# Moving the wait for the gate-bias transfers from behind the first token tile to ahead of the tile loop on VectorE

## The reference, cut to what matters

```
h = rmsnorm(x, norm1_g) * (1 + mod[:, 1]) + mod[:, 0]
p = h @ w_in + b_in            # columns: q, k, v, o (512 each), 16 gates, fourier (512)
...
gates = p[..., OFF_G:OFF_F]    # i and f pre-activations, two directions x four heads
...                            # mLSTM heads, Fourier heads, w_out, expert-choice MoE, final norm
```

## Time and profile before

| what | value |
|---|---|
| median of 3 runs | 2356.2 us (2352.03 to 2357.64) |
| the profiled execution's own time | 2357.64 us |
| its span in the trace | 2355.8 us |
| PE busy | 2190.1 us (93%) |
| DVE busy | 490.4 us (21%) |
| ACT busy | 358.3 us (15%) |
| POOL busy | 271.0 us (12%) |
| mean granted TensorE clock | 0.968 |

### The profile page before, as it was taken

The page is one execution under the profiler, slowest core; times in us unless marked ns, Lnnn a source line. Parts: engine busy times, 40 slices in busy tenths (PEclk is TensorE's granted clock), DMA queues, the critical chain, the costliest instruction groups (busy, mean ns, idle before and its releaser), DMA issues. The chain is left out here.

```text
span 2355.8 us, 37038 instructions
## 1 busy us (share of the span) xinstructions
PE 2190.1 (93%) x15013; PEld 1892.5 (80%) x15013; DVE 490.4 (21%) x1246; ACT 358.3 (15%) x1012; POOL 271.0 (12%) x266
## 2 busy tenths in 40 slices
PE   7999999859985399999999999999999999999992
PEld 2445554846553399999999999999999999999992
DVE  1111115167774410101011101010111011101102
ACT  1011112313321011101111111011111110111102
POOL 0000000011120102022021020120210201202102
PEclk9999999989998699999999999999999999999996
DMA  9720101163422677697797976977979869779775
GB/s 377 294 99 31 62 31 45 72 241 132 137 91 102 205 251 239 245 363 219 277 325 225 345 245 244 363 218 272 330 224 341 250 243 363 218 268 335 224 255 179
DMA packets 351601, 528.76 MB, mean 224 GB/s; under 512 B 12996, under 2 KB 292284, under 8 KB 348232
## 3 DMA queue, kind: packets, MB, share of 16 engines
q1 hardware_dynamic: 336456, 509.35, 62.4%
q0 software_dynamic: 15104, 18.88, 3.9%
HBM read 492.23 MB, written 35.95 MB: 224 GB/s over the span
## 5 line engine op out<-in xcount | busy, mean ns | idle before, releaser
L1626 PE MATMUL ps_ab<-xeT,ring 128*128 128x144 f32 x8192 | 1009.2, 286 | 14.7 <-DVE xeT L1671 14.7
L1626 PEld LDWEIGHTS ps_ab<-xeT,ring 128*128 128x128 f32 x8192 | 1007.5, 190 | 14.8 <-issue 14.8
L1639 PE MATMUL ps_yy<-hidT,ring 128*128 128x144 f32 x4096 | 504.4, 286 | 0.0
L1639 PEld LDWEIGHTS ps_yy<-hidT,ring 128*128 128x128 f32 x4096 | 502.8, 190 | 0.0
L463 PE MATMUL ps_p<-w_in_sb,hT 128*128 128x512 f32 x720 | 318.1, 595 | 3.0 <-DMA w_in_sb<-in_w_in 3.0
L1675 DVE TENSOR_TENSOR hidT<-silu,ps_ab 128x144 f32<-128x144 f32 x256 | 77.8, 304 | 887.0 <-ACT silu L1593 824.7
L463 PEld LDWEIGHTS ps_p<-w_in_sb,hT 128*128 128x128 f32 x720 | 134.6, 191 | 156.6 <-issue 155.5
L1572 POOL DMA_INDIRECT stream<-ye,slot_row x64 | 101.0, 1578 | 1216.5 <-DVE ye_p L1686 1201.9
L1593 ACT ACTIVATE silu<-ps_ab 128x144 f32<-128x144 f32 x256 | 74.5, 291 | 909.8 <-PE ps_ab L1626 884.4
L1215 PE MATMUL b_z<-y,mixT 128*128 128x512 f32 x288 | 129.7, 604 | 10.3 <-ACT aff L1149 10.3
L1679 DVE STREAM_TRANSPOSE yS<-yT 128x1024 f32<-128x1024 f32 x16 | 19.9, 1245 | 457.3 <-ACT yT_p L1600 457.3
(11 more groups left out here) (250 smaller groups left out, 1082.3 us busy)
## 6 DMA issues: line engine op xcount, KB each, us to landing
ring<-in_exp_w SPq DMA_DIRECT2D x384, 1024.0 KB, 12.3
y<-in_ada_w SPq DMA_DIRECT2D x22, 1024.0 KB, 8.1
w_in_sb<-in_w_in SPq DMA_DIRECT2D x4, 2048.0 KB, 21.5
kv<-kvo SPq DMA_DIRECT2D x15, 512.0 KB, 5.7
kvo<-pr SPq DMA_DIRECT2D x9, 768.0 KB, 3.3
qkT_dram<-qkT SPq DMA_DIRECT2D x9, 512.0 KB, 4.8
qk<-qkT_dram SPq DMA_DIRECT2D x9, 512.0 KB, 5.1
m_in<-m_lanes SPq DMA_DIRECT2D x9, 512.0 KB, 5.8
```

What stands on the lines that cost most here:

```text
L1626: mm = nc.tensor.matmul(ps_ab[f % 2][:, N * w:N * w + N], unit[:, k, bass.ts(c, P)], xeT[:, k], start=(k == 0), stop=(k == DT - 1))
L1639: mm = nc.tensor.matmul(ps_yy[d % 2][:, 0:N], unit[:, f % 2, bass.ts(d, P)], hT[:, f], start=(f == 0), stop=(f == FT - 1))
```

## The change

VectorE's wait for the four `b_gate` transfers stood in the body of tile 0, behind its five block additions and just ahead of `keep_gates`. It is taken from there and put ahead of the tile loop, before the wait for `b_in_row`. No instruction is added or removed, and nothing on any other engine or queue is changed.

```diff
                     if only(i, 0):
-                        dve.wait_ge(bg_loaded, 16 * 4)
                         keep_gates()
...
                 keep_shift(ps_ada, 1, 0)
                 g.dve.settle()
                 keep_h(0, 0)
+                dve.wait_ge(bg_loaded, 16 * 4)
                 dve.wait_ge(g.b_in_loaded, 16)
                 tile_loop(dve, g.dve, body, {"hT_ready_dve": 8, "block_kept": 10, "x_normed": 2, "gates_kept": 2})
```

## The result

The changed kernel took 2374.11 us (median of 4 runs, 2371.6 to 2375.61), the kernel before 2354.79 us beside it. The ratio is 1.0081, with a 95% interval of 1.0063 to 1.0098: 0.8% slower, clear of no change. A second set of runs of the same two kernels (in the experiments) gave 1.0067 (1.0050 to 1.0084).

A forecast was written before the change was run, and what follows sets the result against it. The prediction took TensorE's nearly unbroken input projection (1.4 us of waits after 32.09 us) as the bound. Stall 16.4 + clock 2.3 = 18.7 us, on the median 2356.2, gave 2375 us, range 2368 to 2381.

The forecast's parts named there:

- The old place costs nothing: Wait in tile 0's body: keep_gates at 75.03 is released by PE's gate product, so removing the wait gains 0.
- The landing: When the four b_gate transfers on SP's queue have landed: 63.0 us, with 62.5 and 65.4 as ends.
- The group of 46 small packets: Packets under 512 B at 60.2 to 61.0 us, read as the close of the constants together with the four b_gate transfers.
- 2 us behind the closing packets: A transfer counts as landed some 2 us after its closing packets, as the first ada_w slice did at 65.4.
- The stall: PE waits before turn(0) of tile 0 for the first addition: start at 64.0 in place of 47.60, 16.4 us.
- The clock: PE restarts at the lower clock level after the idle time in tile 0: 2.3 us lost, ends 1.6 and 3.0.
- What is late next: SP's first store and the ada_w slices behind it move with the stall; no further cost or gain in the stage: 0.
- The sum: Whole kernel: 16.4 + 2.3 = 18.7 us, forecast 2375 us, 0.8% slower; chance 0.83.
- That small transfers are not held up by the queue: Rival on SP's queue: the four land at 53.1, stall 6.5 us plus 2.3 for the clock, 2365.0 us; chance 0.07.
- That they land with the slices behind them: Rival on SP's queue: completion held up to 72.8 us, stall 26.2 us, time 2384.7 us; chance 0.05.
- The hidden wait: Rival at tile 0's first addition: biases landed by 46.6 us, cost 0, time 2356.2 us; chance 0.03.
- The stall given back: Rival in the stage: something going on during PE's stall absorbs up to 18.7 us; 2373.5 at best, no separate chance.

The follow-up runs named there:

- e7: The kernel before, wait at its old place, with the four bias transfers issued ahead of the w_in blocks; ratio 0.9996.
- e4: The changed kernel with the four bias transfers issued behind the four ada_w slices; ratio 1.0106.
- e5: The changed kernel with the four bias transfers issued just ahead of the 1.5 MB of constants; ratio 1.0053.
- e6: The changed kernel with the bias transfers issued by ACT on its own queue, behind its part of the first hT tile (about 31 us); ratio 0.9996.
- e2: The changed kernel with the wait moved behind the first of the five block additions, so the second is held; ratio 1.0044.
- e3: The changed kernel with the wait moved behind the second of the five block additions, so the third is held; ratio 1.0005.
- e8: The changed kernel with 16 spare 128x512 matmuls, result unread, ahead of turn(0) of tile 0, inside PE's wait; ratio 1.0062.
- e9: The changed kernel with the bias transfers issued by ACT on its own queue only when PE has ended block 1; one run, 2360.86 us.
- e10: The changed kernel run and profiled once more, no edit; ratio to the kernel before 1.0067.
- e1: The changed kernel with the four bias transfers issued ahead of the w_in blocks (about 12.7 us); ratio 0.9996.
- e11: The kernel before run and profiled once more, no edit; one run, 2357.59 us.

## Why the prediction held, point by point

**The old place costs nothing.** Held: `keep_gates` is released by the gate product in both kernels, and in e7 the transfers are issued at 12.6 in place of 50.35 us, with no change of time.

**The landing (forecast 63.0, ends 62.5 to 65.4).** It was 62.1, 0.9 us sooner and below the lower end. The constants landed at 44.41 + 18.4 = 62.8, 0.7 us behind the four small transfers issued after them. The prediction had put them next to the constants and allowed at most 0.5 us for landing ahead. The group of 46 small packets was read rightly: in the changed kernel they come from 60.6 to 61.1, in e4 from 70.5 to 71.0 and in e5 from 57.0 to 57.5, and each time the addition starts some 1.0 to 1.1 us behind them. What was off is the "2 us behind the closing packets", taken from a transfer of 1 MB: it is half of that for the small ones. The groups of e4 and e5:

```profile
DMA packets 50, 0.02 MB, mean 50 GB/s; under 512 B 47, under 2 KB 47, under 8 KB 47
...
DMA packets 101, 0.25 MB, mean 508 GB/s; under 512 B 45, under 2 KB 45, under 8 KB 87
```

That a four-row transfer is split over four engines, with four data and four closing packets, is borne out by e6, where the 32 packets are the only ones of their queue (the Trainium skill, "DMA: Bandwidth & Descriptors", section on why a DMA increments its semaphore by 16).

**The stall (forecast 16.4).** PE's `turn(0)` moved from 47.60 to 62.88, 15.3 us, below the lower end of 15.9. Of the 1.1 us too much, 0.9 are the landing and 0.2 the hand-over: PE followed 0.74 us behind the start of the addition, not 0.94. That it is only the first addition that holds PE is shown by e2 and e3.

**The clock (forecast 2.3, ends 1.6 to 3.0).** `turn(0)` took 1.12 in place of 0.60 and block 2 8.37 in place of 7.03: 1.9 us (1.8 by the starts of the next piece, 9.12 against 7.30 us behind `turn(0)`'s); e8, which takes the idle time away, gives 1.8. The same two pieces lost 1.5 us behind idle times of 7.9 us (e2) and 23.5 (e4), 2.6 behind 10.6 (e5) and 3.0 behind 6.2 (e9). The loss doesn't follow the length of the idle time; it is half of the time for which the clock stays at 0.50 after the restart (the next table). The forecast was the middle of two restarts, and 0.4 too much; its ends hold for the changed kernel, while e2 and e4 lie 0.1 below the lower one. Of the two restarts, the one at 32.09 was read a little low: e8's 32 records at full clock take 13.90 us, not 14.06, so it lost 1.8 and not 1.6.

| run | idle before, us | restart at | clock back at 1.00, about | loss, us |
|---|---|---|---|---|
| changed | 15.0 | 62.88 | 66.5 | 1.8 |
| e10 | 14.9 | 62.80 | 66.7 | 2.0 |
| e2 | 7.9 | 62.75 | 65.7 | 1.5 |
| e4 | 23.5 | 72.76 | 75.7 | 1.5 |
| e5 | 10.6 | 59.27 | 64.4 | 2.6 |
| e9 | 6.2 | 54.03 | 60.0 | 3.0 |

The times of the fourth column are worked out from windows of 1 us, such as these of e4 and e9 (length, busy, clock, DMA share, GB/s):

```profile
75.00:76.00 1.00, 1.00 (x3) 0.67 0.00 0
...
59.00:60.00 1.00, 1.00 (x2) 0.51 1.06 448
```

**What is late next (forecast 0).** Held: no new wait between tile 0 and the end of the stage, L600 17.0 us later and the next stage 17.1 to 17.7 us later. But the prediction had also named as a sign against itself that the distance between the two traces changes by more than 2 us behind tile 0. In the first pair it did, from 17.0 at tile 0 to 13.3 at the end; in the second it did not (16.8 and 16.9).

**The sum (forecast 18.7).** 15.3 + 1.9 = 17.2 us at tile 0, and 17.1 to 17.7 at the end of the stage, in two pairs. The medians give 19.3 and 16.1, since the stretch from the recurrence to the experts varies by some us from execution to execution. The sum was thus 1.5 us too high by the traces: 1.1 in the stall and 0.4 in the clock. The forecast time, 2375, was 0.9 us from the median, and that closeness is partly luck: it counted from 2356.2, where the kernel before had a median of 2354.79 beside the changed one, and the 17.2 us of the traces would give 2372.0. The mechanism was right; the size was off by 1.5 us.

**The rivals.** That small transfers are not held up by the queue falls by the landing at 62.1, and by e4 and e5. That they land with the slices behind them falls too. The hidden wait needs a landing by 46.6; e1 and e6 made it so, and the cost was gone, which bears out that point without fixing it closely. The stall given back: the 4 us of the first pair are not repeated by e10 and e11. A smaller share, of some 2 us, stays open. The stretches above are 2.4 us shorter on average in the kernels that hold PE, but scatter by as much among these, and the medians don't bear it out: against the shift of the next stage's start (from the mean of the five, 424.9) they are between 2.2 us less and 2.3 us more in the six kernels that have a ratio, 0.5 less on average.

## What to carry to other kernels

A wait is priced by two times: when its data lands and when somebody first needs what is queued behind the waiting instruction. Here VectorE was idle for most of the time and the data was not needed for another 30 us, yet the wait cost 0.8%, because TensorE stood behind it; two additions later PE waited 1.1 us, and the run times could not be told from those of before. When a transfer's landing isn't shown, find its packets and the landings of its neighbours on the queue: here a few bytes behind megabytes landed within a microsecond of them, and an earlier issue or another queue cured it, neither at a cost that can be seen.

## What the runs showed of the hardware that was not expected

Small transfers on a queue with nothing ahead of them still took long while SP's large ones kept the DMA engines busy: in e9 the first small packets come 3.7 us after the first issue and the landing is at 5.5 us, and in e6 the first come 3.5 to 3.9 us after it (issue from 29.92, first packets between 33.4 and 33.8). In the idle opening the last small transfer took 1.76 us from issue to use. The Trainium skill ("DMA: Bandwidth & Descriptors", section on queues, rings and completion order) says that each engine takes turns between the queues that have work, a packet at a time. That fits transfers which pass the backlog at some price; how the 3.7 us divide between issue and turns, no run here shows.

The loss to the clock after an idle time was 1.5 to 3.0 us in six restarts, and the longest idle time (23.5 us) had one of the smallest losses, the shortest (6.2 us) the largest. What differed was how long the clock stayed at 0.50 once PE worked again, from 2.9 us (e4) to 6.0 (e9). Busy transfers don't explain it: from 75 to 76 us of e4 none were under way, and the clock was still low for two thirds of that window. What sets the length, no run here shows.
